# mLSTM head norm of a streaming encoder layer: sums of squares by high and low parts, numerator read out in three steps

## The reference, cut to what matters

```
num = S v + w_inter * (q C)                     # 256 values per token
den = sum(S) + w_inter * (q n)
h   = num / max(|den|, exp(-m))
h   = h * rsqrt(mean(h*h over the 256) + eps) * hnorm
y   = h * sigmoid(o) * silu(z)
```

## Time and profile before

| | before |
|---|---|
| median of three runs | 2232.89 us (2232.72 to 2234.09) |
| profiled execution, its span | 2233.14 us, 2231.2 us |
| PE busy | 2217.5 us, 99% |
| DVE, ACT, POOL busy | 1543.5, 944.6, 179.8 us |
| granted PE clock | 0.999 |
| sums of squares on PE (line 1367) | 16 records in the four heads |

### The profile page before, as it was taken

How to read it: one execution, slowest core, us unless ns; L and a number is a source line. 1 busy time by engine, 2 the same in 40 slices (tenths; PEclk the granted TensorE clock), 3 DMA queues, 4 the chain that set the end, 5 groups by cost and what they waited for, 6 DMA issues and landing times.

```text
span 2231.2 us, 39592 instructions
## 1 busy us (share of the span) xinstructions
PE 2217.5 (99%) x16274; PEld 2172.7 (97%) x16274; DVE 1543.5 (69%) x1787; ACT 944.6 (42%) x1274; POOL 179.8 (8%) x238
## 2 busy tenths in 40 slices
PE   9999999999999999999999999999999999999998
PEld 7999999999999999999999999999988999999998
DVE  7876768667666666767666666666678577768676
ACT  5343433334433344444444444444555233224543
POOL 0000000000100000111000000000111112100000
PEclk9999999999999999999999999999999999999999
DMA  6443453534444444444444444444775765763448
GB/s 181 116 129 108 116 144 97 156 99 126 120 127 116 127 116 116 127 116 126 117 125 118 123 120 120 122 118 135 263 225 171 256 189 182 184 173 90 131 130 268
DMA packets 420279, 319.30 MB, mean 143 GB/s; under 512 B 11645, under 2 KB 379653, under 8 KB 418704
## 3 DMA queue, kind: packets, MB, share of 16 engines
q1 hardware_dynamic: 399808, 251.18, 40.9%
q0 software_dynamic: 20224, 65.18, 8.7%
q10 hardware_dynamic: 80, 0.52, 0.1%
HBM read 254.00 MB, written 62.83 MB: 142 GB/s over the span
## 4 chain that ended last, share of the span: by engine, by line
PE 98%; DMA 1%; DVE 0%; ACT 0%; issue 0%; SPq 0%; DVEq 0%; ACTq 0%
PE pp L988 66%; PE pp L1214 13%; PE pp L1402 7%; PE M L1006 2%; PE pp L998 1%; PE M L1318 1%; PE M L1339 1%; PE M L1238 1%; PE pp L1499 1%; PE M L1175 1%; PE M L998 1%; PE M L1267 1%; PE M L1378 1%; DMA gt_lo<-gated_scratch 1%; PE pp L1485 0%; PE M L988 0%
## 5 line engine op out<-in xcount | busy, mean ns | idle before, releaser
L988 PE MATMUL pp<-xa,wa_hi 128*128 128x288 f32 x7392 | 1480.3, 296 | 0.1
L988 PEld LDWEIGHTS pp<-xa,wa_hi 128*128 128x128 f32 x7392 | 1184.9, 188 | 1.1 <-DVE zs L2146 0.4
L988 PE MATMUL pp<-xa,wa_lo 128*128 128x288 f32 x3696 | 1086.7, 294 | 0.0
L988 PEld LDWEIGHTS pp<-xa,wa_lo 128*128 128x128 f32 x3696 | 696.2, 188 | 0.0
L2036 DVE TENSOR_TENSOR wa_lo<-raw_a,wa_hi 128x1024 fp32r<-128x1024 f32 x262 | 326.1, 1248 | 238.7 <-ACT wa_hi L1521 238.6
L1521 ACT ACTIVATE wa_hi<-raw_a 128x1024 fp32r<-128x1024 f32 x262 | 276.6, 1056 | 202.6 <-PE pp L988 201.6
L2036 DVE TENSOR_TENSOR wa_lo<-raw_r,wa_hi 128x1024 fp32r<-128x1024 f32 x134 | 170.7, 1274 | 140.1 <-ACT wa_hi L1521 140.1
L1521 ACT ACTIVATE wa_hi<-raw_r 128x1024 fp32r<-128x1024 f32 x134 | 141.4, 1055 | 133.2 <-PE pp L988 125.9
L1214 PE MATMUL pp<-gt_hi,wb_hi 128*128 128x288 f32 x768 | 169.0, 301 | 0.4 <-DMA gt_lo<-gated_scratch 0.4
L1214 PE MATMUL pp<-gt_hi,wb_lo 128*128 128x288 f32 x768 | 164.5, 296 | 0.0
L1214 PE MATMUL pp<-gt_lo,wb_hi 128*128 128x288 f32 x768 | 164.1, 295 | 0.0
(11 more groups left out here) (374 smaller groups left out, 2580.7 us busy)
## 6 DMA issues: line engine op xcount, KB each, us to landing
raw_a<-in_w_in_dram SPq DMA_DIRECT2D x202, 512.0 KB, 5.0
raw_r<-in_w_in_dram SPq DMA_DIRECT2D x68, 512.0 KB, 5.0
z_scratch<-zs POOLq DMA_DIRECT2D x60, 576.0 KB, 3.3
raw_b<-in_w_branch_dram SPq DMA_DIRECT2D x48, 512.0 KB, 4.7
gz<-z_scratch SPq DMA_DIRECT2D x48, 288.0 KB, 5.2
raw_a<-in_w_out_dram SPq DMA_DIRECT2D x20, 512.0 KB, 6.5
qkv<-z_scratch SPq DMA_DIRECT2D x22, 288.0 KB, 6.0
gt_hi<-gated_scratch SPq DMA_DIRECT2D x4, 1152.0 KB, 7.8
```

The costliest lines, as they stand in the source:

```text
L988: i = nc.tensor.matmul(out, ws[:, slot, k, :], xa[:, o, part, k, :], start=opens and k == 0 and s == 0, stop=k == HK - 1 and s == 2, skip_ ...
```

## The change

The squares are made in two instructions, each after the copy of its own half; their sum over the halves stays in `W_ml`. ACT copies the sum to `q_hi` as fp32r, DVE makes the rest `q_lo` (both lie on the space of `W_ml`). PE multiplies `ones_r` (fp32r) by both parts, four fp32r matmuls in place of two fp32 ones. The sample tokens of `num` are copied first, then each 512-token part by itself.

```diff
--- before.py
+++ after.py
@@ -220,7 +220,7 @@
 def norm_step(i, step):
 
 
-    return 4 * i + step
+    return 5 * i + step
 
 
 def ml_segs(i, step):
@@ -399,6 +399,8 @@
         past_v = sb("past_v", R + 157056, [P, P])
 
         W_ml = sb("W_ml", R + 82944, [P, ML_W])
+        q_lo = sb("q_lo", R + 82944, [P, T], F32R)
+        q_hi = sb("q_hi", R + 82944 + 4 * T, [P, T], F32R)
         states = sb("states", R + 82944, [P, 2 * MC * MDH])
         S_hi = sb("S_hi", R + 88320, [P, ML_W], F32R)
         S_lo = sb("S_lo", R + 93696, [P, ML_W], F32R)
@@ -1362,10 +1364,11 @@
                 m.then_inc(num_done, 1)
                 for h, s in ml_segs(i, 3):
                     seg(h, s)
-                pe.wait_ge(squares_ready, i + 1)
+                pe.wait_ge(squares_ready, 2 * i + 2)
                 for b in range(2):
-                    m = nc.tensor.matmul(M[:, 512 * b:512 * b + TH], ones[:, :], W_ml[:, b * TH:(b + 1) * TH],
-                                         start=True, stop=True)
+                    for s, part in enumerate((q_hi, q_lo)):
+                        m = nc.tensor.matmul(M[:, 512 * b:512 * b + TH], ones_r[:, :], part[:, b * TH:(b + 1) * TH],
+                                             start=s == 0, stop=s == 1)
                 m.then_inc(ssq_done, 1)
                 for h, s in ml_segs(i, 4):
                     seg(h, s)
@@ -1834,10 +1837,13 @@
                     k = MC * i - 1
                     gated_hi(PG + SBH + k, PG + SB_STORED + k, zml[:, 1, :])
                 split_hi(At(h + 4))
-                act.wait_ge(num_ready, 2 * i + 1)
-                nc.scalar.activation(W_ml[:, 0:MC * T].rearrange("p (c t) -> p c t", c=MC), num[:, :, :], ACT.Square
-                                     ).then_inc(norm_act, 1)
-                act.wait_ge(num_ready, 2 * i + 2)
+                for c in range(MC):
+                    act.wait_ge(num_ready, 3 * i + c + 1)
+                    k = nc.scalar.activation(W_ml[:, c * T:(c + 1) * T], num[:, c, :], ACT.Square)
+                k.then_inc(norm_act, 1)
+                act.wait_ge(squares_ready, 2 * i + 1)
+                nc.scalar.activation(q_hi[:, :], W_ml[:, 0:T], ACT.Copy).then_inc(norm_act, 1)
+                act.wait_ge(num_ready, 3 * i + 3)
                 nc.scalar.activation(den[:, :], den[:, :], ACT.Abs).then_inc(norm_act, 1)
                 split_hi(At(h + 5))
                 act.wait_ge(dmax_ready, i + 1)
@@ -2647,23 +2653,25 @@
                 dve.wait_ge(num_done, i + 1)
                 if i:
                     dve.wait_ge(g_ready, PG + SBH + MC * i)
-                nc.vector.tensor_copy(num[:, :, 0:TP], M[:, 0:2 * TP].rearrange("p (c t) -> p c t", c=MC))
-                nc.vector.tensor_copy(num[:, :, TP:T], M[:, 1536:1536 + MC * TS].rearrange("p (c t) -> p c t", c=MC)
-                                      ).then_inc(num_ready, 1)
+                nc.vector.tensor_copy(num[:, :, TP:T], M[:, 1536:1536 + MC * TS].rearrange("p (c t) -> p c t", c=MC))
+                for c in range(MC):
+                    nc.vector.tensor_copy(num[:, c, 0:TP], M[:, c * TP:(c + 1) * TP]).then_inc(num_ready, 1)
                 nc.vector.tensor_copy(den[:, 0:TP], M[:, 1024:1536])
                 nc.vector.tensor_copy(den[:, TP:T], M[:, 1536 + MC * TS:1536 + (MC + 1) * TS]).then_inc(num_ready, 1)
                 dve.wait_ge(norm_act, norm_step(i, 1))
                 nc.vector.tensor_tensor(W_ml[:, 0:T], W_ml[:, 0:T], W_ml[:, T:2 * T], ALU.add).then_inc(squares_ready, 1)
                 dve.wait_ge(norm_act, norm_step(i, 2))
+                nc.vector.tensor_tensor(q_lo[:, :], W_ml[:, 0:T], q_hi[:, :].bitcast(F32), ALU.subtract).then_inc(squares_ready, 1)
+                dve.wait_ge(norm_act, norm_step(i, 3))
                 dve.wait_ge(mem_loaded, 16 * (i + 1))
                 nc.vector.scalar_tensor_tensor(den[:, :], den[:, :], DEN_MIN, EM_h[:, :], ALU.max, ALU.max).then_inc(dmax_ready, 1)
                 split_lo(At(h + 5))
                 merges(i, WEIGH)
                 dve.wait_ge(ssq_done, i + 1)
-                dve.wait_ge(norm_act, norm_step(i, 3))
+                dve.wait_ge(norm_act, norm_step(i, 4))
                 nc.vector.scalar_tensor_tensor(two(den[:, :]), M[:, 0:1024].rearrange("p (b t) -> p b t", b=2)[:, :, 0:TH],
                                                1.0 / MDH, two(den[:, :]), ALU.mult, ALU.add).then_inc(ssq_read, 1)
-                dve.wait_ge(norm_act, norm_step(i, 4))
+                dve.wait_ge(norm_act, norm_step(i, 5))
                 steps.link(nc.vector.reciprocal(den[:, :], den[:, :]))
                 merges(i, SSQ)
                 if i < MLH - 1:
```

## The result

Twenty runs of each kernel: the changed one took 2236.71 us in the median (2233.61 to 2239.28), the one before 2232.82 (2231.85 to 2236.01). The ratio is 1.0017, 95% interval 1.0011 to 1.0023: 3.9 us slower, outside the range that was given (2231.9 to 2236.2), and just inside what is called the same at 0.2%. The single runs also scatter more widely than before. The profiled execution took 2237.97 us, 4.83 more than that of before.

A forecast was written before the change was run, and what follows sets the result against it. PE was taken to bound the kernel (98% of the span). Head 0's -0.44, then +0.41, +1.09, +0.1 and -0.34 summed to +0.8 us: 2233.7 on the median, 2233.9 on the profiled execution; it said 2233.9, range 2231.9 to 2236.2.

The forecast's parts named there:

- Head 2: Sums in head 2: POOL's multiplication holds DVE's addition, PE waits 1.83 us instead of 0.30; +1.09 us.
- head 3: Norm in head 3: DVE's addition starts before POOL's multiplication, PE on time, the read of the sums 0.1 late; -0.34 us.
- head 1: Norm in head 1: POOL holds DVE's addition, the sums wait 0.52 and their read delays PE 0.33; +0.41 us.
- PE's saving: Sums' matmuls on PE: four fp32r take 0.53 us instead of 0.97; 0.44 saved per head, 1.76 in four heads.
- The estimate by the four passes: Sums' matmuls on PE: two fp32 matmuls as eight passes of 0.133, 1.06 us; saving 0.53 per head.
- The way to the sums: From DVE's first copy (t) to PE's sums, unheld: start at t+4.50, 1.04 longer; head 2 then +0.60 us.
- the bound of +3.1: Head 2 at worst: zml's load lands later and POOL holds the addition or subtraction, until t+7; +3.1 us.
- the handover from head 2: Between head 2's state read and the transposes for head 3: DVE's lateness uses up the slack; +0.1 us (0 to 0.4).
- The slow rival: POOL's multiplication holds an addition or subtraction in all of heads 1 to 3; +4.1 us, 2237.0 to 2237.5, chance 0.15.

The follow-up runs named there:

- e1: Changed kernel with POOL's multiplication of zml by oml held back in every head until DVE has read the sums; 2231.76 us, ratio to before 0.9992.
- e8: The changed kernel run again without further edits, on another chip, against its own runs of the kernel before; 2236.76 us, ratio 1.0013.
- e2: Changed kernel with the two fp32 matmuls back and q_hi and q_lo removed, keeping the halved read-out and squares; 2233.40 us, ratio to before 1.0000.
- e7: Kernel before, with POOL's multiplication in head 2 alone made to wait for DVE's copies of the numerator; 2234.38 us, ratio to before 1.0004.
- e3: Changed kernel with the old two-step read-out and single square back, keeping q_hi and q_lo in fp32r; 2239.39 us, ratio to before 1.0026.
- e6: Kernel before, with an unused DVE reciprocal put between the addition and the release of the sums in head 2 alone; 2238.56 us, ratio 1.0025.
- e10: Changed kernel with POOL's multiplication held back until the sums are read, in head 2 alone; 2233.49 us, ratio to before 0.9999.

## Why the prediction was wrong

The heads were forecast to sum to +0.8 us and came to +5.2 in the profiled execution (+3.9 in the median). Head 2 makes 3.1 us of the difference, head 3 1.0 and head 1 0.4.

- **PE's saving** was right in kind and 0.09 short per head: head 0 fell from 14.22 to 13.69, 0.53 and not 0.44. The sums went from 0.97 to 0.54, and the projection half and the state update behind them are 0.07 and 0.03 shorter in the chain as well, which the one row left out. The estimate by the four passes of the Trainium skill ("FP8 and Floating Point Precision", the list that compares precisions) gave a saving of 0.53 as well; the trace agrees with it in the length of the whole head, though not in the sums' own rows.
- **The way to the sums** was right: unheld, in e1, PE's sums begin at t+4.56 (1875.32 less 1870.76, the first copy) for a forecast of 4.50, and head 2 costs +0.67 against the kernel before, for a forecast of +0.60.
- **Head 1** was forecast held and is: +0.82 for +0.41. The wait of the sums was 0.63 for 0.52; the sums' read ended at t+11.07 for 10.95. Most of the rest is that PE's state update takes 3.86 us behind a wait for 3.62 without one, which I left out.
- **Head 2** is the step that failed: the start of POOL's multiplication, put at t+0.2. It began at t+1.78, and the 1.58 us between the two have two parts. The load was issued at t-4.66 and not at t-5.2 (0.54 us), and I took its landing "of this very head", 5.3 us, where it took 6.3 (1.04 us). So the addition ended at t+5.03 and not at t+3.46, and PE waited 3.4 us for 1.83. The 5.3 was not a bad guess, as half of the other profiles show 5.1 to 5.5, but it was one value of a scatter of 4.4 to 7.3. From t+0.2 every longer landing leads to a dearer place; the bound of +3.1 said so, the single value that went into the sum did not.
- **A term was missing**: after a wait of that length the granted clock falls to 0.50. Sums and projection half took 5.46 us (1.33+4.13) where e1 has 3.99 (0.79+3.20): 1.5 us, 2.6 in e8. Wait and clock together make +4.21 for +1.09. I had looked at no row of the clock. No wait of before within the kernel was long enough to move it, but its trace shows the drop at the very end, where PE has run out of work (the page's 0.999 hides it):

```profile
2223.00:2226.00 3.00, 0.63 (x6) 0.43 (x4) 1.75 (x5) 0.68 (x3) 0.00 (x0) 1.00 0.97 295
2226.00:2231.20 5.20, 0.00 (x0) 0.00 (x0) 1.61 (x3) 0.00 (x0) 0.00 (x0) 0.50 0.67 266
```

- **Head 3** was put to DVE by a margin of 0.12 us. It is a race: POOL first in the first profile (+0.71), DVE first in the second (-0.19). The handover from head 2, put at +0.1, cost nothing: the transposes begin 3.18 us behind the state update in both kernels.
- **The slow rival**, POOL in all three heads, is what happened in the profiled execution, at a chance of 0.15; it was priced at 2237.0 to 2237.5, near the median of 2236.71. That its number is so near is in part luck: it has no term for the clock, and its 0.4 for the handover did not come. The forecast had taken the cheaper outcome in heads 2 and 3, both uncertain, and called the two together the likeliest case.

## What to carry to other kernels

In these traces, where two instructions on DVE and POOL both read two inputs from SBUF, whichever began first held the other to its end, and the multiplication that a load releases began anywhere from t-0.6 (e2) to t+1.8 (changed, e7) in head 2. So order such an instruction by a semaphore behind the step that PE waits for, rather than trust that it happened to be out of the way. A longer chain is paid where its cover is shortest; price it head by head. And where the sum of a forecast makes a wait of PE grow, look at what the clock did behind such waits: up to 2.0 us it stayed at 1.00 here, from 3.3 us on it fell, and nothing between was measured.

## What the runs showed of the hardware

- The granted clock of PE stayed at 1.00 behind waits of 1.4 us (e1), 1.8 (e3, profiled execution) and 2.0 (e7), and was 0.50 behind waits of 3.3 (e8), 3.4 (changed) and 4.1 us (e6). In the changed kernel it fell at the end of the wait and stayed low for 3.4 us, which cost 1.5 us; in e8 and e6 it fell some 0.9 and 1.1 us before the wait's end and stayed low for 6.8 us, which cost 2.6 and 2.7 us.
- The hold acts on SCALAR_TENSOR_TENSOR and on an fp32r subtraction as on an addition: 3.18 us instead of 0.75 (e2, head 3), 2.40 instead of 0.76 (e10, head 1). The Trainium skill ("SBUF — State Buffer", SBUF: two separate sides) says that whoever starts first keeps the port pair for the whole instruction; the traces agree in both directions, POOL taking 3.15 and 3.16 us instead of 2.67 where DVE was first.
- Behind a wait the first matmuls of the next group come slower: the state update of 30 matmuls took 3.86 and 3.84 us behind a wait (changed kernel, heads 1 and 3) and 3.58 to 3.62 without. Its first matmul took 0.39 us and the next started 0.22 later, where 0.28 and 0.12 are usual.
- The load of zml in head 2, 576 KB in the same place of the program, landed after 4.4 to 7.3 us in the 13 profiles.
